# Router logits from x before its norm, the choice ahead of the norm's shift, and gate rows through memory, in a two-layer backbone step on one core

## The reference

```python
h = modulate(rmsnorm(xc, norm2_g[l]), sh2, sc2)          # rmsnorm(x) * (1 + sc2) + sh2
logits = (x @ w_router).astype(jnp.float32)              # x is h here
top_v, top_i = lax.top_k(logits, TOP_K)
top_w = jax.nn.softmax(top_v, axis=-1)
y = y + gates[:, e:e + 1] * swiglu(x, we_gate[e], we_up[e], we_down[e])
xc = xc + g2 * y
```

## Time and profile before

| | |
|---|---|
| median of 3 runs | 1332.6 us (1331.96 to 1333.09) |
| profiled execution | 1330.48 us, its span 1328.7 us |
| mean granted TensorE clock | 0.997 of full |
| TensorE busy | 1297.7 us (98%) |
| VectorE, ScalarE, Pool busy | 593.2, 357.5, 131.3 us |
| moved by DMA | 471.41 MB, mean 355 GB/s |
| second layer's routing stage | from the last output products at 427.8 to the first expert product at 449.65 |

### The profile page before, as it was taken

How to read it: one execution, slowest core, us unless ns; L and a number is a source line. 1 busy time by engine, 2 the same in 40 slices (tenths; PEclk the granted TensorE clock), 3 DMA queues, 4 the chain that set the end, 5 groups by cost and what they waited for, 6 DMA issues and landing times.

```text
span 1328.7 us, 28221 instructions
## 1 busy us (share of the span) xinstructions
PE 1297.7 (98%) x12158; PEld 840.7 (63%) x12158; DVE 593.2 (45%) x955; ACT 357.5 (27%) x586; POOL 131.3 (10%) x136
## 2 busy tenths in 40 slices
PE   6999999999999999999999999999999999999996
PEld 4758799998858533456666654545666654556542
DVE  5435755555544514803813732561380381373413
ACT  3334644443434400100700610010160060061001
POOL 0120000000030000000401310000140140131000
PEclk9999999999999999999999999999999999999999
DMA  9999986654693999999999999999999999999991
GB/s 349 361 339 328 359 297 192 192 197 146 259 311 129 421 383 422 384 397 402 421 419 417 420 420 417 420 375 395 408 421 418 419 421 418 417 421 419 417 396 43
DMA packets 113618, 471.41 MB, mean 355 GB/s; under 512 B 10123, under 2 KB 48821, under 8 KB 77654
## 3 DMA queue, kind: packets, MB, share of 16 engines
q1 hardware_dynamic: 111152, 463.80, 88.5%
q10 hardware_dynamic: 1766, 3.70, 0.7%
q0 software_dynamic: 576, 2.10, 0.4%
HBM read 465.43 MB, written 4.13 MB: 353 GB/s over the span
## 4 chain that ended last, share of the span: by engine, by line
PE 92%; DVE 4%; DMA 2%; issue 1%; ACT 1%; POOL 0%; SPq 0%; DVEq 0%; POOLq 0%; ACTq 0%
PE ps L2330 40%; PE ps L2376 18%; PE ps L1917 4%; PE ps L1918 4%; PE ps L1919 4%; PE ps L2345 3%; PE ps L1867 2%; PE ps L1965 2%; DMA token_rows<-y_rows,rti 1%; PE ps L2138 1%; PE ps L2139 1%; PE ps L2140 1%; PE ps L1930 1%; PE ps L1931 1%; PE ps L1932 1%; PE ps L2253 1%
## 5 line engine op out<-in xcount | busy, mean ns | idle before, releaser
L2330 PE MATMUL ps<-ering,xg 128*32 128x512 f32 (+1 forms) x6144 | 585.0, 539 | 1.9 <-DVE sq L1711 1.9
L2330 PEld LDWEIGHTS ps<-ering,xg 128*32 128x32 f32 x6144 | 317.3, 109 | 263.3 <-issue 158.7
L2376 PE MATMUL ps<-ering,eT 128*32 128x512 f32 x1176 | 243.4, 593 | 0.0
L2376 PE MATMUL ps<-wsum,eT 128*32 128x512 f32 x392 | 182.8, 594 | 0.0
L1711 DVE TENSOR_TENSOR sq<-sg,ps 128x512 f32<-128x512 f32 (+1 forms) x48 | 29.7, 619 | 329.3 <-PE ps L2330 245.7
L1121 ACT ACTIVATE sg<-ps 128x512 f32<-128x512 f32 (+1 forms) x48 | 26.1, 544 | 539.0 <-PE ps L2330 539.0
L812 POOL TENSOR_TENSOR sq<-ering 128x512 f32<-128x512 f32 x70 | 96.4, 1377 | 725.3 <-DMA ering<-in_moe_w_down 584.0
L1185 DVE TENSOR_TENSOR low<-ring,high 128x1024 fp32r<-128x1024 f32 (+1 forms) x104 | 122.6, 1202 | 71.5 <-ACT high L851 71.3
L2376 PEld LDWEIGHTS ps<-ering,eT 128*32 128x32 f32 x1176 | 94.4, 110 | 49.1 <-issue 31.7
L1917 PE MATMUL ps<-hx,high 128*128 128x256 f32 x432 | 119.8, 277 | 2.3 <-DVE hx L1239 2.3
L1919 PE MATMUL ps<-hx,low 128*128 128x256 f32 x432 | 119.5, 277 | 0.0
(11 more groups left out here) (295 smaller groups left out, 1622.5 us busy)
## 6 DMA issues: line engine op xcount, KB each, us to landing
ering<-in_moe_w_down SPq DMA_DIRECT2D x112, 1024.0 KB, 13.0
ering<-in_moe_w_gate SPq DMA_DIRECT2D x64, 1024.0 KB, 11.2
ering<-in_moe_w_up SPq DMA_DIRECT2D x64, 1024.0 KB, 13.2
ering<-in_moe_w_gate SPq DMA_DIRECT2D x64, 768.0 KB, 10.2
ering<-in_moe_w_up SPq DMA_DIRECT2D x64, 768.0 KB, 11.6
ring<-in_w_ada SPq DMA_DIRECT2D x40, 1024.0 KB, 7.7
ring<-in_ffn_w_gate SPq DMA_DIRECT2D x11, 1024.0 KB, 6.6
ring<-in_ffn_w_up SPq DMA_DIRECT2D x11, 1024.0 KB, 9.6
```

The costliest lines, as they stand in the source:

```text
L2330: last = mm(ps[32 * c:32 * c + 32, bank, 0:width].rearrange("p (n r) -> p n r", r=64), xg[:, kk, at, 32 * g:32 * g + 32], w[t][:, c, :, :] ...
L2376: last = mm(ps[32 * group:32 * group + 32, bank, :], h, w, start=(n, x) in DOWN_BEGINS, stop=(n, x) in DOWN_ENDS, skip_group_check=True)
```

## The change

The logits are taken apart: with r the reciprocal root of a token, s the scale with its norm gain and t the shift, the logit of h = x r s + t against a router column w is r (x . (s w)) + t . w. VectorE scales the router columns with s, once for each group (`scale_router`), and sums t w over the blocks of channels (`sum_shifts`, ahead of the residual of the last output pair). TensorE multiplies xT, as it is before the norm, with the scaled router (8 columns, token rows out), and sums the shift's part over the partitions with a product of ones. `choose` puts both together and runs the choice ahead of VectorE's half of the shift; its remaining lines are those of 1471 to 1486 of the kernel before, with the difference of the top two at the end.

The x transposes move from ahead of the sums of squares to behind the logits. The gate row is transposed to 8 partitions (two transposes), copied by ScalarE, stored in two further rows of `y_rows`, and loaded on ScalarE's queue with a broadcast to 128 partitions in expert 4; VectorE waits for it ahead of `add_rows`. The 32 gate products, the four gate copies and both `keep_on` are gone. The h transposes go behind the ranks in another order of halves. In both layers ScalarE takes a root of a constant before the squares of the last pair, so that the root's table is loaded there; Exp and Silu of the routing weights move into expert 0, behind the two h2h copies. `GATE_TURNED_BANK` and the new `X_BANK` say which banks are used. ScalarE's three x copies go behind its half of the shift.

```diff
-X_BANK = {(0, 0): 4, (1, 0): 7, (0, 1): 1, (1, 1): 2}
-GATE_BANK = {(0, 0): 3, (0, 1): 5, (1, 0): 6, (1, 1): 0}
+X_BANK = {(0, 0): 4, (1, 0): 7, (0, 1): 6, (1, 1): 3}
+
+H2_ORDER = ((0, 1), (1, 1), (0, 0), (1, 0))
+GATE_TURNED_BANK = 1
+GATE_LOADED = 4
...
+        shifts = view(hid, 0, 2, NE, KD)
+        shift_sums = view(hid, 2 * NE * KD, 2, NE)
+        gate_rows = y_rows[ROWS_KEPT + 1:ROWS_KEPT + 3, :]
+        def router(b):
+            return silu_c[:, :, 2 + NE * b:2 + NE * (b + 1)]
...
@@ ScalarE, mixer(l) @@
                 for j in range(4):
                     upto(min(end("out", l, j) + AHEAD, within("out", l, j)))
+                    if j == 3:
+                        A(stat[:, 30:31], eps[:, 0:1], ACT.Sqrt)
                     squares(2 * l + 1, (j,))
                 take_rows(3 * l + 2)
-                if l:
-                    act.wait_ge(x_router_in, 48)
-                    A(silu_c[:, :, 2:2 + NE], wr[:, :, :], ACT.Copy).then_inc(router_ready, 1)
                 upto(end("gate", 0, 0) if l == 0 else MP0)
                 norm_a(2 * l + 1)
                 if l:
+                    act.wait_ge(gate_turned, 1)
+                    act.wait_ge(stored, 32 * DEPTH)
+                    A(kv_out[0:KD, 0:2 * 128], ps[0:KD, GATE_TURNED_BANK, 0:2 * 128], ACT.Copy).then_inc(gate_row_ready, 1)
+                    act.wait_ge(gate_row_ready, 1)
+                    act.dma_start(gate_rows.rearrange("b (k p) -> k b p", p=128), kv_out[0:KD, 0:2 * 128].rearrange("k (b p) -> k b p", b=2)).then_inc(gate_stored, 16)
+                norm_b(2 * l + 1, l == 0)
+                if l:
                     act.wait_ge(xt_done, 1)
-                    for b, half in ((0, 0), (1, 0), (0, 1)):
+                    for b, half in ((1, 1), (0, 0), (1, 0)):
                         A(xt[:, b, 512 * half:512 * (half + 1)], ps[:, X_BANK[b, half], :], ACT.Copy).then_inc(xt_first_ready, 1)
-                norm_b(2 * l + 1, l == 0)
...
@@ ScalarE, after mixer(1) @@
-            act.wait_ge(gate_done, 2)
-            for b, half in ((0, 0), (1, 1)):
-                A(gate[:, b, 512 * half:512 * (half + 1)], ps[:, GATE_BANK[b, half], :], ACT.Copy).then_inc(gate_first_ready, 1)
...
-            act.wait_ge(top2_ready, 1)
-            A(stat[:, 26:28], stat[:, 24:26], ACT.Exp).then_inc(e1_ready, 1)
-            act.wait_ge(e1_ready, 1)
-            A(stat[:, 28:29], stat[:, 24:25], ACT.Silu).then_inc(esg_ready, 1)
+            for n, (b, half) in enumerate(H2_ORDER):
+                act.wait_ge(h2T_done, n + 1)
+                A(h2[:, b, 512 * half:512 * (half + 1)], ps[:, 2 * b + half, :], ACT.Copy).then_inc(h2_ready, 1)
...
@@ ScalarE, experts(rnd), expert(e), behind take_Y_row(k) @@
+                            if e == GATE_LOADED:
+                                act.wait_ge(gate_stored, 16)
+                                act.dma_start(gate.rearrange("p b d -> p (b d)"), gate_rows.rearrange("b d -> (b d)").rearrange("(o n) -> o n", o=1).to_broadcast([128, 2 * D])).then_inc(gate_in, 16)
...
@@ VectorE, norm_a(t, group) @@
                     take_amod(*divmod(t, 2))
+                if t == 2 * DEPTH - 1:
+                    scale_router()
@@ VectorE @@
+            def sum_shifts():
+                dve.wait_ge(x_router_in, 48)
+                dve.wait_ge(mod_ready, ADA_GROUPS + 2)
+                shift = mod[:, 1, 24:24 + KD, :].rearrange("p k (b o) -> p b o k", o=1).to_broadcast([128, 2, NE, KD])
+                step(V.tensor_tensor(shifts, shift, wr[:, :, :].rearrange("p k (o e) -> p o e k", o=1).to_broadcast([128, 2, NE, KD]), ALU.mult))
+                V.reduce_sum(shift_sums, shifts, AX.X).then_inc(shift_sums_ready, 1)
+            def scale_router():
+                for b in range(2):
+                    factor = amod[:, 1, 1, :, b:b + 1].to_broadcast([128, KD, NE])
+                    last = V.tensor_tensor(router(b), wr[:, :, :], factor, ALU.mult)
+                last.then_inc(router_scaled, 1)
+            def choose():
+                dve.wait_ge(logits_done, 1)
+                lg = stat[:, 32:48].rearrange("p (b e) -> p b e", b=2)
+                step(V.tensor_copy(lg, ps[:, 5, 48:64].rearrange("p (b e) -> p b e", b=2)))
+                for b in range(2):
+                    last = V.scalar_tensor_tensor(lg[:, b, :], ps[:, 5, 32 + NE * b:32 + NE * (b + 1)], rt[:, b:b + 1], lg[:, b, :], ALU.mult, ALU.add)
...
@@ VectorE, mixer(l) @@
+                    if l and j == 3:
+                        sum_shifts()
                     dve.wait_ge(pieces_used, end("out", l, j))
...
                 norm_a(2 * l + 1, 3 * l + 2)
+                if l:
+                    choose()
                 norm_b(2 * l + 1, l == 0)
...
-            b, half = 1, 1
+            b, half = 0, 1
             dve.wait_ge(xt_done, 1)
...
                         if ends:
+                            dve.wait_ge(gate_in, 16)
                             add_rows()
...
@@ TensorE, after mixer(1) @@
+            pe.wait_ge(shift_sums_ready, 1)
+            pe.wait_ge(router_scaled, 1)
+            mm(ps[:, 5, 48:64], ones[:, :], shift_sums.rearrange("p b e -> p (b e)"), start=True, stop=True)
             for b in range(2):
                 for k in range(KD):
+                    last = mm(ps[:, 5, 32 + NE * b:32 + NE * (b + 1)], xT[:, k, b * T:(b + 1) * T], router(b)[:, k, :], start=k == 0, stop=k == KD - 1)
+            last.then_inc(logits_done, 1)
+            pe.wait_ge(mod_ready, DEPTH * ADA_GROUPS)
+            for b in range(2):
+                last = nc.tensor.transpose(ps[0:KD, GATE_TURNED_BANK, b * 128:(b + 1) * 128], mod[:, 1, 40:40 + KD, b], ident)
+            last.then_inc(gate_turned, 1)
+            for k in range(KD):
+                for b in range(2):
+                    last = nc.tensor.transpose(ps[:, X_BANK[b, k // 4], k % 4 * 128:(k % 4 + 1) * 128], xT[:, k, b * T:(b + 1) * T], ident)
+            last.then_inc(xt_done, 1)
             pe.wait_ge(sel_ready, 1)
...
-            keep_on(7, 4, 128)
+            for n, (b, half) in enumerate(H2_ORDER):
+                if n == 0:
+                    pe.wait_ge(h_last_ready, 4)
+                    pe.wait_ge(gate_row_ready, 1)
+                elif n == 1:
+                    pe.wait_ge(xt_first_ready, 1)
+                elif n == 2:
+                    pe.wait_ge(h_ready, 4)
+                for k in range(4 * half, 4 * half + 4):
+                    last = nc.tensor.transpose(ps[:, 2 * b + half, (k % 4) * 128:(k % 4 + 1) * 128], hT[:, k, b * T:(b + 1) * T], ident)
+                last.then_inc(h2T_done, 1)
+            pe.wait_ge(xt_first_ready, 3)
+            pe.wait_ge(xt_last_ready, 1)
```

More of the change, by code:

```diff
@@ L1338, in residual @@
                     dve.wait_ge(x_ready, 4 * (2 * l + i + 2))
+            def sum_shifts():
[15 more added lines that the diff above has]
+                    last = V.scalar_tensor_tensor(lg[:, b, :], ps[:, 5, 32 + NE * b:32 + NE * (b + 1)], rt[:, b:b + 1], lg[:, b, :], ALU.mult, ALU.add)
+                step(last)
+                for b in range(2):
+                    last = V.max(rt8[:, b, :], lg[:, b, :])
+                step(last)
+                for b in range(2):
+                    last = V.max_index(rti[:, b, :], rt8[:, b, :], lg[:, b, :])
+                step(last)
+                step(V.tensor_copy(stat[:, 48:52].rearrange("p (b j) -> p b j", b=2), rti[:, :, 0:2]))
+                iota8 = cst[:, C_IOTA:C_IOTA + NE]
+                for b in range(2):
+                    for j in range(2):
+                        last = V.tensor_scalar(oh[:, j, b, :], iota8, stat[:, 48 + 2 * b + j:49 + 2 * b + j], None, ALU.is_equal)
+                step(last)
+                V.tensor_tensor(oh[:, 2, :, :], oh[:, 0, :, :], oh[:, 1, :, :], ALU.add).then_inc(sel_ready, 1)
+                V.tensor_tensor(stat[:, 24:26], rt8[:, :, 1], rt8[:, :, 0], ALU.subtract).then_inc(top2_ready, 1)
             def mixer(l):
@@ L1682, in experts @@
                     dve.wait_ge(stored, 32 * DEPTH)
+                    dve.wait_ge(gate_stored, 16)
                 def expert(e, begins=False, ends=False):
@@ L2175, in _ @@
             mixer(1)
-            pe.wait_ge(mod_ready, DEPTH * ADA_GROUPS)
-            for i, ((b, half), bank) in enumerate(GATE_BANK.items()):
-                if bank == 0:
-                    pe.wait_ge(normed, 2 * (2 * DEPTH - 1) + 2)
-                for k in range(4 * half, 4 * half + 4):
-                    row = mod[:, 1, 40 + k, b:b + 1].to_broadcast([128, 128])
-                    last = mm(ps[:, bank, k % 4 * 128:(k % 4 + 1) * 128], row, ident, start=True, stop=True)
-                if i % 2:
-                    last.then_inc(gate_done, 1)
```

68 lines of the change are left out of this document (10 added, 58 removed).

## The result

The changed kernel took 1335.76 us (median of 16, 1333.59 to 1337.5) against 1331.98 for the kernel before (median of 16, 1330.91 to 1333.38): +3.78 us, ratio 1.0027 with the interval 1.0020 to 1.0034. The range held it; the forecast did not.

The account below looks back on a forecast made before the run. TensorE, busy 98% of the span, bounds the kernel; the routing stage's chain of waits sets the gather. Gather -1.0, table -0.15, clock spell +1.5 sum to +0.35: 1332.95 us, range 1330.4 to 1336.0.

Parts of the forecast that it names:

- the clock term: Routing stage: nearly column-free products and waits without fillers drop TensorE's clock for one spell on the path, costing 1.5 us.
- the logits: Routing stage on TensorE: 17 narrow calls take 3.6 us, up to 5.0, ending at 436.65.
- the slower rival: Routing stage: logits run at the low clock level, 5.7 us instead of 3.6; +2.95 in all, 1335.55 us; chance 0.18.
- second spell on the gather: Part of the slower rival: the clock falls again before the gather into expert 0, +1.5 us.
- fillers at no price: Routing stage: six filling products vanish with no cost charged; their absence is mentioned only among the clock's conditions.
- ScalarE's chain: Routing stage: gate copy and store, shift, x copies, then four h2 copies to 444.85 set the gather's start at 444.9.
- the choice: VectorE behind the logits: 0.5 us of copy and fused operations, then 1.65, giving sel_ready at 438.9.
- the call price of 0.21: TensorE's narrow logits: 0.21 us a call, taken from the sums of squares' 1.70 us for 8 calls.
- the predicted gain of 1.0: Routing stage: the gather of expert 0 starts at 444.9 instead of 445.87, 1.0 us earlier.
- The table: First layer on ScalarE: loading the root's table early gains 0.15 us, at most 0.17; second layer zero.
- The gate load: Expert 4, ScalarE's queue: the 1 MB load of gate rows costs nothing; 2.4 us without cover, a rival with chance 0.05.
- The moved exponential and Silu loads: ScalarE in expert 0: table loads of 1.28 us each lie beside its first products, zero cost; 2.6 without cover.

Follow-up runs that it names:

- 1: Changed kernel with eight wide filling products of 128 columns among its logits, one behind every second router call: 1338.17 us, ratio 1.0049 to the kernel before.
- 3: Changed kernel with the two gate transposes ahead of the logits and one x transpose ahead of each router call: 1333.62 us, ratio 1.0018 to the kernel before.
- 12: Changed kernel with the 16 x transposes back ahead of the sums of squares, two banks changed to suit: 1338.02 us, ratio 1.0056 to the kernel before.
- 8: Changed kernel with logits in the old form, 32 router columns stationary and x moving, 8 calls: 1329.36 us, ratio 0.9996 to the kernel before.
- Experiment 5: Kernel before without its six filling products around the ranks, nothing else changed: 1334.53 us, ratio 1.0024 to the kernel before.
- 6: Kernel before with only the root's table loaded early, by a root of a constant, in both layers: 1330.86 us, ratio 0.9997 to the kernel before.
- 4: Changed kernel with the 1 MB load of gate rows in expert 4 replaced by one tiny copy: 1334.64 us, ratio 1.0022 to the kernel before.
- 10: Run 9 plus the second half of expert 7's row adding put behind its first step's products: 1328.13 us, ratio 0.9964 to the kernel before.
- 7: Changed kernel with the second half of expert 7's row adding put behind its first step's products: 1331.94 us, ratio 1.0002 to the kernel before.
- 2: Changed kernel with only the two gate transposes moved ahead of the logits: 1333.72 us, ratio 1.0016 to the kernel before.
- 9: Run 8 plus ten filling products in TensorE's two waits, behind the x transposes and ahead of the gather: 1329.58 us, ratio 0.9982 to the kernel before.

## Why the prediction went wrong

**What failed: the clock term.** The prediction put the likeliest spell of 1.5 us "where it reaches work on the path (gate transposes, gather, first expert products)" and kept the logits at 3.6. In the profile the fall came within the logits: they took 5.6, and the transposes behind them 1.1 more than in their old place, while the gather ran at 1.00. That is the slower rival's first part (5.7 for the logits), on which I had put 0.18, arguing that the wide products before 433 spoke for a high level. The profiles of experiments 1, 3 and 12 show how little wide products helped there; 8 shows that the form of the logits is worth 4.1 us, of which the low level is only a part: at the high one the narrow calls would take 3.6 us (the prediction's term), against 1.07 for the wide ones. The rival's second spell on the gather was absent from this profile; one came in expert 7 instead, behind the wait.

**How far the range was luck.** The median lies 0.24 us inside the upper end, and 7 of the 16 executions lie above it. That end was the slower rival's sum and half a microsecond, and of the sum only the logits' part came true in the profile; its other part, a second spell on the gather, was replaced by the wait and fall in expert 7, which no rival had.

**What failed beside it: fillers at no price.** The prediction let six filling products "vanish" and gave them only a word among the conditions of the clock. Experiment 5 prices their removal alone at 3.0 us. These prices don't add up to the total (the early root and choice give some back, and a fall can be charged but once), but each by itself is about as large as the whole loss: some three microseconds had been bought by products that compute nothing.

**What held.** From the gate copy on, ScalarE's chain went as worked out, only later: forecast 437.0 for the copy's start, 438.0 for the shift, 444.85 for the end of the fourth h2 copy; measured 439.62, 440.44 and 446.99, so 2.6, 2.4 and 2.1 late. The late start is the logits' 2.0 and some 0.6 of handing over (their start at 433.41 and not 433.0, and the way from their end to ScalarE's copy). Copy and store took 0.82 against 1.0. The root came at 431.76 (forecast 431.55), the scaling took 0.36 (0.45), the choice 2.3 (2.15, with 1.65 put in for a row of 1.79), places for expert 0 came before they were needed, and the call price of 0.21 from the sums of squares was right at the high level. The late start turns the predicted gain of 1.0 into a gather 1.38 later.

**The small terms.** The table: 0.07, not 0.15. It is not the 1.5 either that I estimated from the extra drain in the Trainium skill, "ScalarE: Activation LUTs", section "What ACT_TABLE_LOAD costs" (6). The gate load: nothing that could be measured (4). The moved exponential and Silu loads, at 451.68 and 453.20, stand off the path.

**What was not in it at all.** Expert 7's wait was in the trace of before and bounds both kernels. I had read the stage and the weights' reserve, and asked only whether weights would be late. Removing it gives 2.7 to 3.3 us in either, nearly as much as the change costs.

**Left open.** Why the clock falls in one execution and not in the next; why the stores and gathers of rows in expert 7 take 7.6 to 8.1 and 8.6 to 10.0 us, and why 2.08 us pass ahead of Pool's second gather in one chain and 3.62 in the other; 0.4 us in the last combine; whether the 2.9 us in the routing stage would divide between logits and missing fillers, for no kernel had the change with its narrow logits and fillers in the two waits alone.

## What to carry to other kernels

Where a small operand meets a wide one, keep the small one stationary and let the wide one move: a chain of products with 8 moving columns cost 5.6 us for what took 1.07 the other way round, partly by calls and partly because the clock fell in it. The wide form needs a copy, two transposes and a sum besides; with them the stage from the sums to the gather was still 4.15 us shorter (8). Price a removed filling product by an experiment or by the low-level rows, never at nothing. And before counting a gain at an early stage, follow the chain to its end: a wait near the end that both kernels have may be worth as much as the change.

## What the runs showed of the hardware that I had not expected

Once down, the clock stayed at 0.50 for some 3.5 us in the profiles of 5, 6 and 10, for 7 in the changed kernel's and 10 in those of 4 and 7, and for 13.5 to 17 us in those of 1, 2, 3 and 12. In the second, TensorE was busy without a break for the 14.00 us from 435.5 to 449.5, and the granted clock of that stretch was 0.51. Weight loads of 128 columns follow each other at 0.10 us at the high level and 0.20 at the low one. One kernel spread over 9.5 us (3), the longest ones at the lower mean clocks, while the slowest execution of another was 1337.12 us without fillers in two waits and 1331.59 with them (8 and 9).
